# Forgetting attention: scores from three F32R products instead of one float32 product, keys before queries, and eight projection steps before the first row's scores instead of six

## The reference

```
q = rms_norm(q.reshape(B, S, FOX_HEADS, FOX_DH), q_norm_g)      # 16 heads of 64
k = rms_norm(k.reshape(B, S, FOX_HEADS, FOX_DH), k_norm_g)
...
logits = jnp.einsum('bhtd,bshd->bhts', qb, kf) + cb[..., None] - c_t[:, :, None, :]
logits = jnp.where(key_pos[None, :] <= q_pos[:, None], logits, -jnp.inf)
probs = jax.nn.softmax(logits, axis=-1)
return jnp.einsum('bhts,bshd->bthd', probs, vf)
```

## Time and profile before

| | |
|---|---|
| median of three runs | 1759.19 us |
| span of the profiled execution | 1755.8 us, 28773 instructions |
| PE busy | 1687.5 us, 96% |
| weight loads (PEld) | 1287.9 us, 73% |
| DVE, ACT, POOL busy | 50%, 45%, 18% |
| the attention of the eight pairs | from about 1103 to 1529 us, some 53.8 us a pair |
| part of the DMA engines' time in use by the data queue | 18.5% |

### The profile page before, as it was taken

One profiled execution on the slowest core, in us unless ns is written; L12 is line 12 of the kernel. 1 busy time (PEld: TensorE's weight loads), 2 busy tenths in 40 slices (PEclk: granted clock), 3 DMA queues, 4 the chain that ended last, 5 costly groups with the idle time before them and its releaser, 6 DMA issues. The chain is left out here.

```text
span 1755.8 us, 28773 instructions
## 1 busy us (share of the span) xinstructions
PE 1687.5 (96%) x11157; PEld 1287.9 (73%) x11157; DVE 882.0 (50%) x1655; ACT 788.9 (45%) x1288; POOL 312.6 (18%) x243
## 2 busy tenths in 40 slices
PE   9999999999999899799999999999999999899898
PEld 6777777777777677678777887666666665688686
DVE  5757667575666635854322200344444544577533
ACT  4746556464554722142222311556555665531411
POOL 5213212132222251300000000222221221013000
PEclk9999999999999999999989999999999999999999
DMA  6202011210102122051130202111111101051411
GB/s 158 62 26 49 13 50 22 52 37 25 50 13 57 41 97 72 13 168 46 39 110 26 71 2 45 40 45 31 46 35 42 43 22 43 2 175 40 144 46 51
DMA packets 115574, 94.42 MB, mean 54 GB/s; under 512 B 19760, under 2 KB 97776, under 8 KB 115440
## 3 DMA queue, kind: packets, MB, share of 16 engines
q1 hardware_dynamic: 115440, 92.59, 18.5%
HBM read 84.08 MB, written 8.49 MB: 53 GB/s over the span
## 5 line engine op out<-in xcount | busy, mean ns | idle before, releaser
L435 PE MATMUL gdn_unit<-part_hi,gdn_w_hi 128*128 128x512 f32 x496 | 225.7, 455 | 0.0
L437 PE MATMUL gdn_unit<-part_hi,gdn_w_lo 128*128 128x512 f32 x496 | 195.3, 394 | 0.0
L436 PE MATMUL gdn_unit<-part_lo,gdn_w_hi 128*128 128x512 f32 x496 | 194.0, 391 | 0.0
L2108 DVE CUSTOM_DVE_ANT_0 fa_probs<-fa_scores,fa_decay 128x896 f32<-128x896 f32 (+7 forms) x128 | 97.0, 758 | 120.9 <-PE fa_scores L1920 73.6
L867 DVE SCALAR_TENSOR_TENSOR x<-gdn_raw,gdn_taps,x 128x512 f32<-128x512 f32 x144 | 129.4, 899 | 24.3 <-ACT x L665 19.4
L399 POOL TENSOR_TENSOR gdn_w_lo<-ring,gdn_w_hi 128x1024 fp32r<-128x1024 f32 x31 | 75.2, 2427 | 250.7 <-ACT gdn_w_hi L645 250.7
L2054 ACT ACTIVATE fa_probs_t<-fa_turned 128x512 f32<-128x512 f32 (+1 forms) x96 | 52.3, 545 | 139.0 <-PE fa_turned L1937 138.4
L2048 ACT ACTIVATE fa_probs<-fa_probs,fa_top 128x896 f32<-128x896 f32 (+7 forms) x128 | 99.4, 777 | 22.1 <-DVE fa_top L2108 18.4
L437 PEld LDWEIGHTS gdn_unit<-part_hi,gdn_w_lo 128*128 128x128 f32 x496 | 93.1, 188 | 21.0
L435 PEld LDWEIGHTS gdn_unit<-part_hi,gdn_w_hi 128*128 128x128 f32 x496 | 93.7, 189 | 16.1 <-issue 3.6
L1295 PE MATMUL e_gate<-e_w_hi,part_hi 128*128 128x512 f32 x256 | 101.8, 398 | 3.0 <-DVE part_lo L1430 2.8
(11 more groups left out here) (329 smaller groups left out, 3681.0 us busy)
## 6 DMA issues: line engine op xcount, KB each, us to landing
ring<-in_gdn_w_in_dram SPq DMA_DIRECT2D x31, 512.0 KB, 4.1
ring<-in_ple_w_gate_dram SPq DMA_DIRECT2D x32, 256.0 KB, 3.2
ring<-in_fox_w_in_dram SPq DMA_DIRECT2D x32, 256.0 KB, 3.1
ring<-in_fox_w_in_dram SPq DMA_DIRECT2D x16, 512.0 KB, 4.7
fa_decay<-c_rows_scratch SPq DMA_DIRECT2D x64, 128.0 KB, 3.0
gdn_g_bc<-g_rows_scratch SPq DMA_DIRECT2D x8, 512.0 KB, 8.9
x_scratch<-x SPq DMA_DIRECT2D x8, 512.0 KB, 2.9
m_old<-x_scratch SPq DMA_DIRECT2D x8, 512.0 KB, 3.5
```

The source lines that it names most:

```text
L435: pe.matmul(out, w_hi[:, j % 2, k, :], xh[:, k, ts], start=(k == 0), stop=False)
L436: pe.matmul(out, w_hi[:, j % 2, k, :], xl[:, k, ts], start=False, stop=False)
L437: mm = pe.matmul(out, w_lo[:, j % 2, k, :], xh[:, k, ts], start=False, stop=(k == KT - 1))
L2108: step(dve.tensor_tensor_reduce(probs[:, n % 3, blocks(e)], scores[head][:, blocks(e)], decay[:, head, blocks(e)], 1.0, 3e38, ALU.add, ALU ...
```

## The change

Four things. (1) Kind 0 is now the keys and kind 1 the queries, in the loads of the weights, the gains and the tiles. (2) `qk` is no longer kept twice (for odd and even pairs); after the normalisation it is split into `qk_hi` (a copy by ACT that rounds to F32R) and `qk_lo` (the difference, by DVE). This is done in three parts: all keys; the last 128 queries, which row 0 needs; the other 896 queries. (3) The scores are three F32R products (hi·hi, hi·lo, lo·hi) in place of one float32 product. (4) Eight steps stand before the scores of row 0 and two behind them. The scratch for dynamic DMAs of the program is made smaller (`dynamic_dma_scratch_size=1024`), to find room for the tiles; no DMA of the page is issued by POOL.

```diff
-AHEAD_OF_SCORES = 6
+AHEAD_OF_SCORES = 8
...
-        qk = sb("qk", [P, 2, 2, T])
+        qk = sb("qk", [P, 2, T])
+        qk_hi, qk_lo = sb("qk_hi", [P, 2, T], F32R), sb("qk_lo", [P, 2, T], F32R)
...
+        def parts(kind):
+
+            return (slice(0, T),) if kind == 0 else (slice(T - P, T), slice(0, T - P))
...
         @block.tensor
...
             def score(p, e):
                 n, i = 2 * NT * p + 2 * e, row(e)
-                if e == 0:
-                    pe.wait_ge(normed, 2 * p + 2)
-                else:
+                if e:
 
                     pe.wait_ge(topped, n)
-                width = (i + 1) * P
+                pe.wait_ge(split_low, 3 * p + min(e, 1) + 2)
+                width, own = (i + 1) * P, slice(i * P, (i + 1) * P)
                 for at in range(0, width, HALF):
                     end = min(width, at + HALF)
-                    for head in range(2):
-                        rows = slice(head * DH, (head + 1) * DH)
-                        mm = pe.matmul(scores[head][:, at:end], qk[rows, p % 2, 0, i * P:(i + 1) * P],
-                                       qk[rows, p % 2, 1, at:end], start=True, stop=True)
-                        if end == width:
-                            mm.then_inc(scored, 1)
+                    for term, (a, b) in enumerate(((qk_hi, qk_hi), (qk_hi, qk_lo), (qk_lo, qk_hi))):
+                        for head in range(2):
+                            rows = slice(head * DH, (head + 1) * DH)
+                            mm = pe.matmul(scores[head][:, at:end], a[rows, 1, own], b[rows, 0, at:end],
+                                           start=(term == 0), stop=(term == 2))
+                            if end == width and term == 2:
+                                mm.then_inc(scored, 1)
...
                     if e == 0:
-                        fill(4)
+                        fill(2)
...
         @block.scalar
...
                 act.wait_ge(unit_made, n + 1)
-                step(act.activation(qk[:, it % 2, u // 2, u % 2 * HALF:(u % 2 + 1) * HALF], unit_bank(it, u), ACT.Copy),
+                if it:
+
+                    act.wait_ge(split_low, 3 * it - (2 if u < 2 else 0))
+                step(act.activation(qk[:, u // 2, u % 2 * HALF:(u % 2 + 1) * HALF], unit_bank(it, u), ACT.Copy),
                      unit_taken)
...
+            def split(p, kind, part):
+                n, ts = kind + part, parts(kind)[part]
+                act.wait_ge(normed, 3 * p + n + 1)
+                if p:
+
+                    act.wait_ge(scored, 2 * NT * p)
+                step(act.activation(qk_hi[:, kind, ts], qk[:, kind, ts], ACT.Copy), split_high)
...
                     root(p, 0)
                     root(p, 1)
+                    split(p, 0, 0)
+                    split(p, 1, 0)
+                    split(p, 1, 1)
                 fill(AHEAD_OF_SCORES)
...
-                        fill(4)
+                        fill(2)
...
         @block.vector
...
+            def normalise(p, kind, part):
+                ts = parts(kind)[part]
+                dve.wait_ge(roots, 2 * p + kind + 1)
+                step(dve.scalar_tensor_tensor(qk[:, kind, ts], qk[:, kind, ts], gains[:, kind:kind + 1],
+                                              squares[kind][:, ts], ALU.mult, ALU.mult), normed)
+
+            def low_part(p, kind, part):
+                n, ts = kind + part, parts(kind)[part]
+                dve.wait_ge(split_high, 3 * p + n + 1)
+                step(dve.tensor_tensor(qk_lo[:, kind, ts], qk[:, kind, ts], qk_hi[:, kind, ts].bitcast(F32),
+                                       ALU.subtract), split_low)
...
-                for kind in range(2):
-                    dve.wait_ge(roots, 2 * p + kind + 1)
-                    step(dve.scalar_tensor_tensor(qk[:, p % 2, kind], qk[:, p % 2, kind], gains[:, kind:kind + 1],
-                                                  squares[kind], ALU.mult, ALU.mult), normed)
+                normalise(p, 0, 0)
+                normalise(p, 1, 0)
+                low_part(p, 0, 0)
+                low_part(p, 1, 0)
+                normalise(p, 1, 1)
+                low_part(p, 1, 1)
...
-    nc = _bacc.Bacc("TRN2", target_bir_lowering=False, num_devices=1)
+    nc = _bacc.Bacc("TRN2", target_bir_lowering=False, num_devices=1, dynamic_dma_scratch_size=1024)
```

More of the change, by code:

```diff
@@ L1723, in fox_attention @@
         summed, roots, normed = sem("summed"), sem("roots"), sem("normed")
+        split_high, split_low = sem("split_high"), sem("split_low")
         masked, scored, topped, exped = sem("masked"), sem("scored"), sem("topped"), sem("exped")
@@ L1752, in heads_half @@
         def heads_half(p, kind, head, half):
-            return qk[head * DH:(head + 1) * DH, p % 2, kind, half * HALF:(half + 1) * HALF]
+            return qk[head * DH:(head + 1) * DH, kind, half * HALF:(half + 1) * HALF]
+        def parts(kind):
+            return (slice(0, T),) if kind == 0 else (slice(T - P, T), slice(0, T - P))
         def turn_order(e):
@@ L1772, in columns @@
         def columns(j):
-            pair, kind = j // 2, j % 2
-            return slice(kind * WIDTH + pair * P, kind * WIDTH + (pair + 1) * P)
+            pair, at = j // 2, (1 - j % 2) * WIDTH
+            return slice(at + pair * P, at + (pair + 1) * P)
         def blocks(e):
@@ L1799, in load_decay @@
                 sp.dma_start(decay[:, :, i * P:(i + 1) * P], pair.partition_broadcast(P)).then_inc(d_loaded[i], 16)
-            for n, g in enumerate((q_gain, k_gain)):
+            for n, g in enumerate((k_gain, q_gain)):
                 for head in range(2):
@@ L2136, in _ @@
             dve.wait_ge(small, 64)
-            step(dve.tensor_scalar(gains[:, 0:1], gains[:, 0:1], -DH ** -0.5, None, ALU.mult))
+            step(dve.tensor_scalar(gains[:, 1:2], gains[:, 1:2], -DH ** -0.5, None, ALU.mult))
             for it in range(1, PAIRS + 2):
@@ L2194, in build_program @@
                                  for n in range(4)])
-        to_attention = ahead("fa", columns(fox_in, (0, WIDTH)))
+        to_attention = ahead("fa", columns(fox_in, (WIDTH, 0)))
         with ExitStack() as gdn:
```

## The result

The changed kernel takes 1803.55 us (median of four runs, 1802.7 to 1807.55); the kernel before took 1759.22 beside it (1757.87 to 1759.38). The ratio is 1.0263 (1.0249 to 1.0278): 44 us slower, where the prediction had 1805 us. The profiled execution was the slowest of the four. Its span is 50.0 us over that of the profile before. From the sums of squares of one pair to those of the next, the seven pairs with a projection beside them lie 42.8 us further apart in total, and the last pair's values come another 4.4 us later; the other 2.8 us lie in stretches outside the attention. So the attention alone is 47.2 us longer in this execution, where the medians differ by 44.3.

A forecast was written before the change was run, and what follows sets the result against it. PE, busy 96% of the span, was taken as the bound. Seven pairs losing 4.6 us to waits and 1.4 to clock (42.0), plus 3.8 in the last, made 45.8 on 1759.2: 1805 us, range 1784 to 1822.

The forecast's parts named there:

- The first wait: PE ahead of step 8 stands 4.0 us for ACT's copy of the unit, queued behind ACT's third copy.
- The second wait: PE ahead of row 1 waits about 1.3 us for DVE; row 1 starts 4.9 us late.
- The last pair: Pair without copy of the unit: row 1 2.7 us late, clock 1.4, less 0.3 for rows: 3.8 us lost.
- The rows' gain: Three F32R products instead of one float32 in rows 1 to 7: 0.3 us gained a pair, 128-column pieces costing 0.64 us.
- The clock: PE's granted clock falls to 0.50 in each pair after the 4.0 us idle: 1.4 us, between 0 and 1.7.
- The loads: Weight loads of the scores, three times a half row and head instead of twice: hidden by matmuls, cost nothing.
- the third rival: Score products not side by side, or their loads bare: 49 to 54 us more, up to 1859 us; 8%.
- The first rival: PE's clock holds: 1794 us, or 1787 if narrow products run at the projection's pace too; 15%.
- The second: Rival: copies on ACT and DVE estimated too high, first wait 1 to 2.5 us less, no clock fall: 1774 to 1786; 11%.
- The fourth: Rival: copy of the unit ready when step 8 comes, PE never stands: 1747 to 1754 us; 4%.

The follow-up runs named there:

- the run with the whole normalisation and six and four: Changed kernel with queries normalised in one instruction ahead of the subtractions, and six steps ahead of row 0, four behind: 1759.56 us, ratio 1.0008.
- the run with dummies: Changed kernel with 16 matmuls of 512 columns on useless data ahead of step 8 in the seven pairs with projection: 1791.27 us, ratio 1.0195.
- the kernel with the whole normalisation and eight and two: Changed kernel with queries normalised in one instruction ahead of the three subtractions, counts left at eight and two: 1773.56 us, ratio 1.0087.

## Why the prediction was right, point by point

**The first wait** was predicted at 4.0 us, ahead of step 8 and released by ACT's copy of the unit; it was 3.93 in six pairs and 4.59 in the first. The chain behind it (third high part, normalisation of 896 columns, two subtractions) is that of the working, and undoing either end of it, the counts or the order on DVE, took the long wait away.

**The second wait** was predicted at about 1.3 us and was 0.89 to 1.12. DVE's last subtraction (done at 1176.87) does not touch it, as was worked out.

**The last pair**: row 1 was predicted 2.7 us late. From the sums of squares it came 14.74 us on instead of 12.10, so 2.64. Its wait was 3.16 us, and the clock was low behind it:

```profile
1538.64 0.79 PE L1926 MATMUL fa_scores<-fa_qk_hi 64*128 64x512 f32 x2 [3.16 <-DVE fa_top L2140]
```

```profile
1538.60:1540.60 2.00, 1.96 (x10) 1.67 (x12) 0.00 (x0) 1.29 (x3) 0.41 (x1) 0.50 0.00 0
```

From row 1 to its last values the pair took 39.39 us, against 36.77 in the run with the whole normalisation and six and four, which has the same products at a clock of 1.00 there. So the fall cost 2.6 us where 1.4 was taken, and the pair ended 4.4 us late instead of 3.8.

**The rows' gain** was mis-sized: the step that let the two 128-column pieces run at the pace of float32, at 0.64 us each. The timeline of PE in the row of 640 columns:

```profile
1197.27 0.39 PE L1926 MATMUL fa_scores<-fa_qk_hi,fa_qk_lo 64*128 64x512 f32 x2
1197.49 0.22 PE L1926 MATMUL fa_scores<-fa_qk_hi 64*128 64x128 f32 x2
1197.55 0.28 PE L1926 MATMUL fa_scores<-fa_qk_lo,fa_qk_hi 64*128 64x128 f32 x2
1197.66 0.28 PE L1926 MATMUL fa_scores<-fa_qk_hi,fa_qk_lo 64*128 64x128 f32 x2
```

Full-speed narrow products start 0.11 us apart, so the three take 0.33 us, neither 0.171 nor 0.64. From row 1 to the next sums of squares a pair took 40.23 us (the third pair) instead of 41.21: the gain is 0.98 us, where 0.3 was predicted, and 26 x 0.043 - 2 x (0.33 - 0.214) = 0.9 gives it. Over seven pairs this is 5 us in the kernel's favour.

**The clock** was mis-sized the other way: a fall in each pair was predicted, at 1.4 us; the run with dummies gives 2.0, above even the upper bound of 1.7. Seven times 0.6 is 4 us. The step at fault took the length of the low stretch from the windows of two places, 2 and 3 us, as if the fall lasted no longer; here it lasted up to six us of work. One of the two places was also no clean case of a fall after 2.19 us: its trace has an idle time of 3.40 us just ahead, with only 1.9 us of work between. So the total owes some of its closeness to two errors of 4 to 5 us that cancel. The pair came out at +6.1 us against +6.0.

**The loads** were costed at nothing, and cost nothing. Timeline of the weight loads in the row above:

```profile
1197.03 0.19 PEld L1926 LDWEIGHTS fa_scores<-fa_qk_hi,fa_qk_lo 64*128 64x128 f32 x2
1197.27 0.19 PEld L1926 LDWEIGHTS fa_scores<-fa_qk_hi 64*128 64x128 f32 x2
```

Two loads, one a head, run while the products of 1197.03 and 1197.27 do, and pairs of products start every 0.23 us. Consecutive products of one head use the same row group, so a load does not need another row group to be hidden, and the third rival falls. The Trainium skill ("TensorE: Matmul & The Clock Gate", Part 3, the mechanism) does state the rule that the prediction drew on, that a load overlaps matmuls in flight only if its row group differs; this trace does not agree, with 0.23 us between the starts. The same section of the Trainium skill also names a background weight buffer as a second way for a load to be pulled ahead; that would fit, but no run here shows where a load goes. The first rival (clock holds) fell in all seven pairs. The second fell with the 3.93 us. The fourth, on the other side, would have needed the copy in time; it was already late without the splits.

**Not settled:** why the profiled execution is 50.0 us longer, 2.8 of them outside the attention, where the medians differ by 44.3 (the four runs of the changed kernel lie up to 4.9 us apart); why the low clock begins sooner or later after the same idle time; and what besides its length decides whether it comes at all.

## What to carry to other kernels

When work is moved from behind a consumer to ahead of it, ask which copy used to pass under the thing it overtakes: here a single PSUM bank made the moved steps wait for ACT, and fewer steps were left to cover DVE behind the scores; the two waits cost 15 us before anything else was changed. When a new operation is split into pieces to start its first consumer sooner, follow the last piece too: what is queued behind it on each engine waits for the whole chain. Two changes that cost 14 and 15 us one by one cost 44 together here, mostly because the clock of PE fell after the longer wait that they made.

## What the runs showed of the hardware

A pair of F32R products of 64 rows, one a head, starts every 0.23 us for 512 columns, 0.18 for 384, 0.12 for 256 and 0.11 for 128: below 256 columns the pace hardly gains. Of the seven waits of step 8 in the kernel with the whole normalisation and eight and two, the five of 1.71 to 1.73 us kept the clock, and those of 2.00 and 2.39 us were followed by a fall, at a price of 1.5 us for the one of 2.00 (57.40 - 55.64, less the 0.27 us that the wait was longer). But the kernel with the whole normalisation and six and four shows a shorter wait with a fall, in its first pair, and a longer one without, in its last; their rows on PE, and a window behind each:

```profile
1112.82 0.51 PE L1926 MATMUL fa_scores<-fa_qk_hi 64*128 64x512 f32 x2 [1.88 <-DVE fa_qk_lo L2127]
...
1490.86 0.50 PE L1926 MATMUL fa_scores<-fa_qk_hi 64*128 64x512 f32 x2 [2.58 <-DVE fa_qk_lo L2127]
```

```profile
1114.80:1116.80 2.00, 2.00 (x6) 1.49 (x5) 1.61 (x3) 0.32 (x1) 2.00 (x1) 0.50 0.00 0
...
1490.80:1492.80 2.00, 1.94 (x14) 1.37 (x15) 1.25 (x3) 0.00 (x0) 0.00 (x0) 1.00 0.00 0
```

So the length of one idle time does not decide alone. In the six pairs of the changed kernel whose idle time was 3.93 us, the clock fell each time, but before the restart in one pair and after it in the next: the traces show pairs of 60.4 and 59.4 us taking turns.
